# Two pieces of prompt work, then two value tiles, in the value pass of an attention kernel

## The chip, the cores and the metric

The kernel runs on one core of a Trainium2 chip. The metric is the device time in microseconds (us) of one execution, all inputs and outputs in the chip's memory. TensorE (PE) does the matrix products, with its weight loads shown apart as PEld; VectorE (DVE), ScalarE (ACT) and GpSimd (POOL) do the rest; SyncE (SP) and ACT issue the transfers (DMA) that the change touches. The engines run in order, each its own list of instructions, and wait for each other on semaphores.

## The reference

The reference is one step of a two-layer decoder: a diagonal state-space layer, then a layer of sparse attention, for a prompt of 256 tokens and for 8 samples of one token each. Only the attention is touched. It has 16 heads of 128 in 4 groups, and three branches that are weighted by gates: compressed keys, selected blocks, and a window.

```python
def nsa_mixer(hn, pos, kv, w_q, w_gate, b_gate, w_o):
    ...
    o_cmp, p_grp = cmp_branch(q, pos, kv['k_cmp'], kv['v_cmp'])
    idx, ok = select_blocks(p_grp, pos, kv['n_slc'])
    o_slc = kv['slc_fn'](q, pos, idx, ok)
    o_win = kv['win_fn'](q, pos)
    o = gates[:, :, 0] * o_cmp + gates[:, :, 1] * o_slc + gates[:, :, 2] * o_win
    return o.reshape(bsz, t, N_HEADS * HEAD_DIM) @ w_o
```

Each branch is a masked softmax: scores of the queries against the keys, less their maximum, exponential, divided by the sum, times the values. All is float32.

## The kernel before, in words

The attention runs two jobs at once. The samples' job streams the cached keys, then the cached values, through a ring of slots in on-chip memory: a tile is 128 rows of 1024 numbers, 512 KB. The value pass has 84 tiles, t = 80 to 163, or v = 0 to 83: 16 of the window, 64 of selected pages, 4 of compressed values. `values_pe` multiplies one tile: 8 instructions, each with 4 columns of probabilities as its weights and 128 columns of values moving, four of them side by side for the four groups (L2486). The trace counts two records for each of these instructions, 16 for a tile.

The prompt's job is cut into 24 items k: two halves of the queries (items 0 to 11, and 12 to 23), four groups, three branches. Items with k divisible by 3 have 15 compressed keys; the others have 128 keys in the first half and 256 in the second. An item passes through the engines in this order:

- scores on PE, `prompt_scores_pe`, L2303;
- on DVE the mask and the negative maximum, `prompt_mask_dve`, L2347 to L2355;
- on ACT four exponentials, `prompt_exp_act`, L2391;
- on DVE the probabilities, `prompt_probs_dve`, L2366 to L2377;
- on PE the turning of the probabilities, `prompt_turn_pe`, L2317;
- on ACT their copy out of PSUM, `prompt_take_act`, L2400;
- on PE the outputs, `prompt_outputs_pe`, L2329, and after each third item a copy on DVE, L2383.

The order of all this is written out by hand with v as the beat. In `beside_values_pe`, beat v = 3k has the scores of item k + 2, beat 3k + 1 turns item k, beat 3k + 2 has the outputs of item k - 1. Six extra pieces of the samples' job stand at v = 6, 8, 9, 16, 22 and 28. DVE has the probabilities of item k + 1 at beat 3k and then the mask of item k + 2 at beat 3k + 1. ACT has at beat 3k + 2 first the copy of item k, then the exponentials of item k + 2; behind every beat it issues half of the load that goes into the slot which tile v leaves, and for that it waits until PE has done tile v (`att_used`). SP issues the other half. Scores of item k wait until the mask of the item that last used their PSUM bank has read it, which for the items of 256 keys and those behind them is item k - 1.

The ring has 11 slots. The last four tiles, t = 160 to 163, come from a scratch tensor (L2051), all issued by SP, into the slots that tiles 150 to 153 leave; the first weight slab of the output projection is issued by SP between t = 160 and t = 161. Then the accumulated sample outputs are turned (L2593) and the output projection begins (L429).

Of the kernel before, what the change touches and what calls it, by code (L numbers as in the profile page):

```python
# [20 lines left out]
D, TP, TS, DEPTH = 2048, 256, 8, 2  # L21
# [88 lines left out]
def trunk_kernel(nc, io, out):  # L110
# [1863 lines left out]
    WK, SK, WV, SV, CV, TILES = 0, 16, 80, 96, 160, 164  # L1974
    SV_ALL = WV
# [31 lines left out]
    def tile_slot(t):  # L2007
        return TILE_SLOT[t]
# [50 lines left out]
    def wait_tile(pe, t):  # L2059
        done, base = TILE_READY[tile_slot(t)]  # L2060
        pe.wait_ge(done, base + 32 * (TILE_TURN[t] + 1))
# [19 lines left out]
    def gates_pe(pe):  # L2081
        pe.wait_ge(wg_split, 1)
        pe.wait_ge(free_a, by_name["o"].groups)
        for k in range(KC):
            if k == 10:
                own_rows_pe(pe)
            nc.tensor.matmul(PSUM[:, GATE_BANK, 0:T], WGH[:, k, :], XH[:, k, :], start=k == 0, stop=False)
            nc.tensor.matmul(PSUM[:, GATE_BANK, 0:T], WGH[:, k, :], XL[:, k, :], start=False, stop=False)
            last = nc.tensor.matmul(PSUM[:, GATE_BANK, 0:T], WGL[:, k, :], XH[:, k, :], start=False, stop=k == KC - 1)
        last.then_inc(gates_done, 1)  # L2090
# [202 lines left out]
    def prompt_scores_pe(pe, k):  # L2293
        qt, g, br = item = ITEMS[k]
        if k == 0:
            pc_dve.wait(pe, "k rows")
            pc_act.wait(pe, "v rows")
            pe.wait_ge(rope_done, len(ROPED))
        elif scores_before(k):
            pe.wait_ge(sc_used, scores_before(k))  # L2300
        for r in range(HREP):
            keys = KCP[:, g * NCMPP:(g + 1) * NCMPP] if br == 0 else KVT[:, 2 * br, g, 0:keys_of(item)]
            last = nc.tensor.matmul(score_view(k)[:, r, :], QT[:, HREP * g + r, qt * P:(qt + 1) * P], keys, start=True, stop=True)  # L2303
        last.then_inc(sc_done, 1)
# [6 lines left out]
    def prompt_turn_pe(pe, k):  # L2311
        pe.wait_ge(pr_done, k + 1)
        if k >= 1:
            pe.wait_ge(pt_taken, k)
        for kc, w in parts_of(k):
            for r in range(HREP):
                last = nc.tensor.transpose(PSUM[0:w, PROBS_BANK + kc, r * P:(r + 1) * P], prompt_rows(k)[:, r, kc * P:kc * P + w], IDENT[:, :])  # L2317
        last.then_inc(pt_done, 1)

    def prompt_outputs_pe(pe, k):  # L2320
        qt, g, br = ITEMS[k]
        parts = parts_of(k)
        pe.wait_ge(pt_taken, k + 1)
        o = k // 3
        if br == 0 and o >= 1:
            pe.wait_ge(po_used, o)
        for kc, w in parts:
            v = VCP[0:w, g, :] if br == 0 else VNAT[0:w, br - 1, kc, g * DH:(g + 1) * DH]
            last = nc.tensor.matmul(PSUM[:, OUT_BANK, :], v, PTP[0:w, k % 2, kc, :], start=br == 0 and kc == 0,  # L2329
                                    stop=br == 2 and kc == len(parts) - 1)  # L2330
        last.then_inc(pv_done, 1)
# [62 lines left out]
    def prompt_take_act(act, k):  # L2394
        n = keys_of(ITEMS[k])
        act.wait_ge(pt_done, k + 1)
        if k >= 2:
# [11 lines left out]
    sp_act = Steps("sp_act", ["cmp exp", "cmp turned kept", "block scores kept", "cmp gated kept", "win exp", "win new exp",  # L2409
                              "slc exp", "slc new exp", "slc kept 0", "slc kept 2"])  # L2410
    sp_dve = Steps("sp_dve", ["cmp negmax", "cmp probs", "new taken", "sums taken", "cmp gated", "win negmax", "win probs",
                              "win kept", "slc negmax", "slc probs", "new probs", "new kept", "new added",
                              "slc kept 1", "slc kept 3", "out"])
    ch_dve = sem("ch_dve")
    chain = [0]
    KSTEPS, VSTEPS = SV_ALL - WK, TILES - SV_ALL
# [10 lines left out]
    def turn_pe(pe, u):  # L2427

        wait_tile(pe, WK + u)
        if u == 1:  # L2430
            pe.wait_ge(gate_sig, 1)
            pe.wait_ge(part_done, 1)
        for e in range(2):
            if u >= 2:
                pe.wait_ge(kt_taken[e], u - 1)
            for g in range(G):
                at = 512 * e + g * DH
                last = nc.tensor.transpose(PSUM[:, 2 * (u % 2) + e, g * P:(g + 1) * P], TILE[:, tile_slot(WK + u), at:at + DH], IDENT[:, :])  # L2438
            last.then_inc(att_used, 1)
# [37 lines left out]
    def values_pe(pe, t):  # L2477
        wait_tile(pe, t)
        for e in range(2):
            if t < CV:  # L2480
                m, b = divmod(t - (WV if t < SV else SV), TS)
                probs, rows = (STW if t < SV else SCT)[:, 2 * m + e, :], P
            else:
                b, probs, rows = 2 * (t - CV) + e, PCS[0:NCMP, 2, :], NCMP
            for g in range(G):
                last = nc.tensor.matmul(PSUM[ROWS * g:ROWS * g + HREP, ACC_BANK + b // 4, b % 4 * P:(b % 4 + 1) * P],  # L2486
                                        probs[:, ROWS * g + HREP * b:ROWS * g + HREP * (b + 1)],
                                        TILE[0:rows, tile_slot(t), 512 * e + g * DH:512 * e + (g + 1) * DH],
                                        start=False, stop=False, skip_group_check=True)
            last.then_inc(att_used, 1)  # L2490
# [45 lines left out]
    def beside_values_pe(pe, v):  # L2536

        k, stage = divmod(v, 3)
        if stage == 0 and k + AHEAD_OF_VALUES < len(ITEMS):
            prompt_scores_pe(pe, k + AHEAD_OF_VALUES)  # L2540
        if stage == 1 and k < len(ITEMS):
            prompt_turn_pe(pe, k)
        if stage == 2 and 1 <= k <= len(ITEMS):
            prompt_outputs_pe(pe, k - 1)
        if v == 6:
            sp_dve.wait(pe, "new probs")
            for k in range(2):
                last = nc.tensor.transpose(PSUM[0:32, SPARE_BANK, k * P:(k + 1) * P], RTW[:, k, :], IDENT[:, :])
            sp_pe.made_by(last, "new turned")
        if v == 8:  # L2550
            sp_dve.wait(pe, "new kept")
            for k in range(2):
                last = nc.tensor.matmul(PSUM[:, SPARE_BANK, 2 * P:3 * P], SNAT[:, 3 + 2 * k, :], RTK[0:32, k, :], start=k == 0, stop=k == 1)
            sp_pe.made_by(last, "new values")
        if v in TURNED_AT:
            q = TURNED_AT.index(v)
            if q == 0:
                sp_dve.wait(pe, "new added")
            elif q % 2:
                sp_act.wait(pe, f"slc kept {q - 1}")  # L2560
            else:
                sp_dve.wait(pe, f"slc kept {q - 1}")
            for j in range(4):
                last = nc.tensor.transpose(PSUM[:, SPARE_BANK, j * P:(j + 1) * P], S2[:, (4 * q + j) * P:(4 * q + j + 1) * P], IDENT[:, :])
            sp_pe.made_by(last, f"slc turned {q}")

    def attention_pe(pe):
        gates_pe(pe)
        compressed_scores_pe(pe)
        turn_pe(pe, 0)  # L2570
        for u in range(KSTEPS):
            if u + 1 < KSTEPS:
                turn_pe(pe, u + 1)
            scores_pe(pe, u)
            beside_keys_pe(pe, u)
        pe.wait_ge(sc_used, AHEAD_OF_VALUES)
        for bank in range(2):
            nc.tensor.matmul(PSUM[:, ACC_BANK + bank, :], ZERO[:, 0:P], ZERO[:, :], start=True, stop=False, skip_group_check=True)
        for e in range(2):
            pe.wait_ge(kt_taken[e], KSTEPS)  # L2580
        for v in range(VSTEPS):
            t = SV_ALL + v
            beside_values_pe(pe, v)
            if t == WV:
                sp_dve.wait(pe, "win kept")
            if SV <= t < CV and (t - SV) % (2 * TS) == 0:
                q = (t - SV) // (2 * TS)
                (sp_dve if q % 2 else sp_act).wait(pe, f"slc kept {q}")
            values_pe(pe, t)
        for b in range(TS):  # L2590
            if b % 4 == 0:
                pe.wait_ge(vo_taken[b // 4], 1)
            last = nc.tensor.transpose(PSUM[:, b // 4, b % 4 * P:(b % 4 + 1) * P], VO[:, b // 4, b % 4 * P:(b % 4 + 1) * P], IDENT[:, :])  # L2593
        sp_pe.made_by(last, "out turned")
# [559 lines left out]
```

## Time and profile before

| what | value |
|---|---|
| median of 3 runs | 3226.36 us (3226.16 to 3226.61) |
| the profiled execution, its own time | 3226.72 us |
| its span in the trace | 3224.7 us |
| PE busy | 3167.0 us, 98% of the span |
| DVE busy | 1994.4 us, 62% |
| ACT busy | 1553.1 us, 48% |
| value pass, first piece to last value tile | 2107.2 to 2239.3 us in the span |

Times inside the trace count from the start of the span. A row of the timeline gives the start, the busy time, the engine with its line, and how many records were merged into it. A matrix product's busy time overlaps the next one's, so the distance from one start to the next is what a group costs.

### The profile page before, as it was taken

What the parts mean: (1) busy time and instruction counts of PE and PEld (TensorE: products, weight loads), DVE (VectorE), ACT (ScalarE), POOL (GpSimd) and SP (SyncE); (2) the same over time, 40 slices, a digit from 0 to 9 for tenths busy, and PEclk for the clock granted to TensorE, in tenths of its full rate; (3) what the DMA queues carried; (4) which work ended last, traced back from release to release, by engine and by line L of the source; (5) the groups of instructions that cost most, each with busy time, mean ns of one, the idle gap of its engine ahead of it and who ended that gap; (6) DMA issues with size and microseconds to landing.
All of it is one profiled execution on the core that took longest, in us unless ns stands there. A gap on an engine that the chain in (4) does not pass through costs nothing.

```text
span 3224.7 us, 68739 instructions
## 1 busy us (share of the span) xinstructions
PE 3167.0 (98%) x27708; PEld 3034.7 (94%) x27708; DVE 1994.4 (62%) x2283; ACT 1553.1 (48%) x1929; POOL 520.4 (16%) x476
## 2 busy tenths in 40 slices
PE   7999999999999999999999999999999999999998
PEld 6999899899999999999999997866999999999998
DVE  7998888865655544555675546465655554555566
ACT  4555555644544444444554533354554444444454
POOL 5666666600000000000000006000000000000000
PEclk9999999999999999999999999999999999999999
DMA  6455555466565556665556659898556555656553
GB/s 183 150 160 163 164 157 155 136 188 185 171 193 181 183 183 191 181 183 184 181 183 183 183 179 314 282 353 264 181 182 183 175 190 182 183 176 189 183 181 127
DMA packets 384389, 608.39 MB, mean 189 GB/s; under 512 B 52537, under 2 KB 144987, under 8 KB 383883
## 3 DMA queue, kind: packets, MB, share of 16 engines
q1 hardware_dynamic: 351738, 539.06, 53.5%
q10 hardware_dynamic: 29392, 60.86, 5.5%
q0 software_dynamic: 3024, 5.22, 0.5%
q8 instruction: 162, 2.65, 0.3%
q14 instruction: 73, 0.59, 0.1%
HBM read 594.83 MB, written 26.94 MB: 193 GB/s over the span
## 4 chain that ended last, share of the span: by engine, by line
PE 93%; DVE 3%; issue 1%; ACT 1%; DMA 1%; POOL 1%; SPq 0%; DVEq 0%; ACTq 0%; POOLq 0%
PE psum L429 23%; PE psum L431 23%; PE psum L430 23%; PE psum L1081 4%; PE psum L1082 3%; PE psum L1083 3%; PE psum L1060 3%; PE psum L2438 2%; PE psum L2448 1%; PE psum L2486 1%; PE psum L1138 1%; PE psum L2303 1%; PE psum L2329 1%; ACT state_ri L1226 1%; PE psum L2317 0%
## 5 line engine op out<-in xcount | busy, mean ns | idle before, releaser
L396 DVE TENSOR_TENSOR w_rest<-w_raw,w_head 128x1024 fp32r<-128x1024 f32 x776 | 973.0, 1265 | 945.3 <-ACT w_head L392 944.4
L392 ACT ACTIVATE w_head<-w_raw 128x1024 fp32r<-128x1024 f32 x776 | 909.6, 1183 | 945.4 <-PE psum L431 936.0
L429 PE MATMUL psum<-act_head,w_head 128*128 128x264 f32 x4224 | 1205.2, 285 | 1.6 <-DVE act_rest L2896 1.6
L431 PE MATMUL psum<-act_head,w_rest 128*128 128x264 f32 x4224 | 1200.9, 284 | 0.0
L430 PE MATMUL psum<-act_rest,w_head 128*128 128x264 f32 x4224 | 1199.9, 284 | 0.0
L429 PEld LDWEIGHTS psum<-act_head,w_head 128*128 128x128 f32 x4224 | 821.9, 195 | 2.4 <-issue 2.0
L430 PEld LDWEIGHTS psum<-act_rest,w_head 128*128 128x128 f32 x4224 | 822.4, 195 | 0.1
L431 PEld LDWEIGHTS psum<-act_head,w_rest 128*128 128x128 f32 x4224 | 821.8, 195 | 0.0
L429 PE MATMUL psum<-hid_head,w_head 128*128 128x264 f32 x1408 | 400.6, 284 | 0.0
L431 PE MATMUL psum<-hid_head,w_rest 128*128 128x264 f32 x1408 | 399.9, 284 | 0.0
L430 PE MATMUL psum<-hid_rest,w_head 128*128 128x264 f32 x1408 | 399.5, 284 | 0.0
L1819 POOL TENSOR_TENSOR hid_rest<-prod_val,hid_head 128x1056 f32 x22 | 54.4, 2471 | 1717.9 <-ACT hid_head L1780 1717.9
L1081 PE MATMUL psum<-rows_head,w_head 128*128 128x256 f32 x1024 | 301.3, 294 | 12.0 <-ACT state_ri L1226 5.1
L1082 PE MATMUL psum<-rows_rest,w_head 128*128 128x256 f32 x1024 | 290.9, 284 | 0.0
L1083 PE MATMUL psum<-rows_head,w_rest 128*128 128x256 f32 x1024 | 290.8, 284 | 0.0
L430 PEld LDWEIGHTS psum<-hid_rest,w_head 128*128 128x128 f32 x1408 | 273.7, 194 | 0.0
L429 PEld LDWEIGHTS psum<-hid_head,w_head 128*128 128x128 f32 x1408 | 273.5, 194 | 0.0
L431 PEld LDWEIGHTS psum<-hid_head,w_rest 128*128 128x128 f32 x1408 | 273.5, 194 | 0.0
L1217 ACT ACTIVATE rows_head<-psum 128x512 fp32r<-128x512 f32 x256 | 139.7, 596 | 209.0 <-PE psum L1060 208.9
L1081 PEld LDWEIGHTS psum<-rows_head,w_head 128*128 128x128 f32 x1024 | 194.8, 190 | 19.9 <-DVE rows_rest L1385 10.6
L1082 PEld LDWEIGHTS psum<-rows_rest,w_head 128*128 128x128 f32 x1024 | 195.3, 191 | 0.0
L1083 PEld LDWEIGHTS psum<-rows_head,w_rest 128*128 128x128 f32 x1024 | 195.2, 191 | 0.0
(433 smaller groups left out, 3990.4 us busy)
## 6 DMA issues: line engine op xcount, KB each, us to landing
w_raw<-in_ffn_w_gate SPq DMA_DIRECT2D x176, 512.0 KB, 4.4
w_raw<-in_ffn_w_up SPq DMA_DIRECT2D x176, 512.0 KB, 4.5
w_raw<-in_ffn_w_down SPq DMA_DIRECT2D x176, 512.0 KB, 3.7
w_raw<-in_cache_cmp_k SPq DMA_DIRECT2D x256, 128.0 KB, 2.6
w_raw<-in_cache_cmp_v SPq DMA_DIRECT2D x256, 128.0 KB, 2.6
w_raw<-in_ssm_w_glu SPq DMA_DIRECT2D x64, 512.0 KB, 4.4
w_raw<-in_ple_w_gate SPq DMA_DIRECT2D x64, 512.0 KB, 4.1
w_raw<-in_kv_w SPq DMA_DIRECT2D x48, 512.0 KB, 3.8
```

The source lines that it names most:

```text
L392: nc.scalar.activation(pairs(WH, u), tiles_of(RAW, u), ACT.Copy).then_inc(head_done, 1)
L396: nc.vector.tensor_tensor(pairs(WL, u), tiles_of(RAW, u), pairs(WH, u).bitcast(F32), ALU.subtract).then_inc(rest_done, 1)
L429: nc.tensor.matmul(o, wh, head, start=k == 0, stop=False)
L430: nc.tensor.matmul(o, wh, rest, start=False, stop=False)
L431: last = nc.tensor.matmul(o, wl, head, start=False, stop=k == UK * kunits - 1)
L1060: last = nc.tensor.transpose(PSUM[:, n % 2, q * P:(q + 1) * P], RAW[:, u, 256 * q + g * DH:256 * q + (g + 1) * DH], IDENT[:, :])
L1081: nc.tensor.matmul(o, WH[:, part, w], hi, start=t == 0, stop=False)
L1082: nc.tensor.matmul(o, WH[:, part, w], lo, start=False, stop=False)
L1083: last = nc.tensor.matmul(o, WL[:, part, w], hi, start=False, stop=t == TAPS - 1)
L1217: nc.scalar.activation(head_rows(k, m // 2, m % 2), page_rows(n), ACT.Copy).then_inc(cmp_head, 1)
L1819: nc.gpsimd.tensor_tensor(HL[:, ds(4 * i, 4), :], ZB[:, :, :], HH[:, ds(4 * i, 4), :].bitcast(F32), ALU.subtract).then_inc(hl_done, 1)
L2438: last = nc.tensor.transpose(PSUM[:, 2 * (u % 2) + e, g * P:(g + 1) * P], TILE[:, tile_slot(WK + u), at:at + DH], IDENT[:, :])
```

## The change

Only PE's order in the value pass changes. Before, each beat was one beat's pieces, then one tile. Now two beats' pieces come first, and then both tiles. What PE waits for ahead of each tile stays with the tile. The lists of ACT, DVE, SP and POOL are as before.

```diff
-        for v in range(VSTEPS):
-            t = SV_ALL + v
+        for v in range(0, VSTEPS, 2):
             beside_values_pe(pe, v)
-            if t == WV:
-                sp_dve.wait(pe, "win kept")
-            if SV <= t < CV and (t - SV) % (2 * TS) == 0:
-                q = (t - SV) // (2 * TS)
-                (sp_dve if q % 2 else sp_act).wait(pe, f"slc kept {q}")
-            values_pe(pe, t)
+            beside_values_pe(pe, v + 1)
+            for t in (SV_ALL + v, SV_ALL + v + 1):
+                if t == WV:
+                    sp_dve.wait(pe, "win kept")
+                if SV <= t < CV and (t - SV) % (2 * TS) == 0:
+                    q = (t - SV) // (2 * TS)
+                    (sp_dve if q % 2 else sp_act).wait(pe, f"slc kept {q}")
+                values_pe(pe, t)
```

The first place is the middle of the second half, beats 50 to 53, on PE. `x8` of L2486 is one tile; L2329 is an outputs piece, L2303 scores, L2317 turning. Before:

```order
L2329 MATMUL psum<-probs_t_p,v_cmp_p 128x512
L2486 MATMUL psum<-tiles,scores_st 4x128 x8
L2303 MATMUL psum<-kv_t,q_t 128x256 x4
L2486 MATMUL psum<-tiles,scores_st 4x128 x8
L2317 MATMUL psum<-ident,scores_p_149 128x128 x8
L2486 MATMUL psum<-tiles,scores_st 4x128 x8
L2329 MATMUL psum<-probs_t_p,v_rows 128x512 x2
L2486 MATMUL psum<-tiles,scores_st 4x128 x8
```

The same beats on PE after the change:

```order
L2329 MATMUL psum<-probs_t_p,v_cmp_p 128x512
L2303 MATMUL psum<-kv_t,q_t 128x256 x4
L2486 MATMUL psum<-tiles,scores_st 4x128 x16
L2317 MATMUL psum<-ident,scores_p_149 128x128 x8
L2329 MATMUL psum<-probs_t_p,v_rows 128x512 x2
L2486 MATMUL psum<-tiles,scores_st 4x128 x16
```

The tile of beat 52 stood right behind the turning piece (L2317) of its own beat; now an outputs piece (L2329 x2) stands between them. The tile of beat 50 now stands behind the scores of beat 51.

The second place is the end of the pass on PE, from the turning of item 22 on, as a difference:

```order
 L2317 MATMUL psum<-ident,scores_p 128x128 x8
 L2486 MATMUL psum<-tiles,scores_st 4x128 x8
+L2486 MATMUL psum<-tiles,scores_st 4x128 x16
 L2329 MATMUL psum<-probs_t_p,v_cmp_p 128x512
 L2486 MATMUL psum<-tiles,scores_st 4x128 x16
 L2317 MATMUL psum<-ident,scores_p_149 128x128 x8
-L2486 MATMUL psum<-tiles,scores_st 4x128 x8
 L2329 MATMUL psum<-probs_t_p,v_rows 128x512 x2
-L2486 MATMUL psum<-tiles,scores_st 4x128 x24
+L2486 MATMUL psum<-tiles,scores_st 4x128 x32
 L2329 MATMUL psum<-probs_t_p,v_rows 128x512 x2
```

Tile 150, whose slot takes t = 160, moves from ahead of the outputs of item 22 to behind them. In the whole pass the tiles stood in 70 runs between pieces; now they stand in 37.

## Rows read from the trace of the kernel before

**Rows 1.** Busy time by stretch, core 0: length, busy of each engine, PEclk, DMA share, GB/s.

```profile
2108.00:2228.00 120.00, 119.23 (x1565) 73.10 (x1563) 73.53 (x193) 57.23 (x211) 0.00 (x0) 1.00 0.93 325
...
2244.00:2249.00 5.00, 5.00 (x24) 5.00 (x24) 4.44 (x9) 5.00 (x12) 0.00 (x0) 0.50 0.48 170
```

**Rows 2.** Timeline of PE late in the pass: start, busy, engine, line, out<-in, records.

```profile
2218.67 1.06 PE L2486 MATMUL psum<-tiles,scores_st 128*4 128x128 f32 x32
2219.66 1.09 PE L2317 MATMUL psum<-ident,scores_p 128*128 128x128 f32 x8
2220.68 0.62 PE L2486 MATMUL psum<-tiles,scores_st 128*4 128x128 f32 x16
2221.23 1.12 PE L2329 MATMUL psum<-probs_t_p,v_cmp_p 15*128 15x512 f32 x2
```

**Rows 3.** Timeline of PE early in the pass, two turning pieces.

```profile
2116.84 0.66 PE L2317 MATMUL psum<-ident,scores_p 128*128 128x128 f32 x4
2117.42 0.62 PE L2486 MATMUL psum<-tiles,scores_wt 128*4 128x128 f32 x16
...
2130.91 0.66 PE L2317 MATMUL psum<-ident,scores_p 128*128 128x128 f32 x4
2131.40 0.60 PE L2564 MATMUL psum<-ident,scores_s 128*128 128x128 f32 x4
```

**Rows 4.** Timeline of DVE: masks of items 4, 7, 13 to 16, 23; last probabilities.

```profile
2119.01 0.68 DVE L2347 TENSOR_TENSOR scores_p<-psum,causal 128x512 f32<-128x512 f32 x1
...
2131.44 0.68 DVE L2347 TENSOR_TENSOR scores_p<-psum,causal 128x512 f32<-128x512 f32 x1
...
2158.74 1.22 DVE L2347 TENSOR_TENSOR scores_p<-psum,causal 128x1024 f32<-128x1024 f32 x1
...
2165.32 1.22 DVE L2347 TENSOR_TENSOR scores_p<-psum,causal 128x1024 f32<-128x1024 f32 x1
...
2171.89 0.21 DVE L2347 TENSOR_TENSOR scores_p<-psum,cmpvis 128x60 f32<-128x60 f32 x1
...
2175.16 1.22 DVE L2347 TENSOR_TENSOR scores_p<-psum,causal 128x1024 f32<-128x1024 f32 x1
...
2216.24 1.22 DVE L2347 TENSOR_TENSOR scores_p<-psum,causal 128x1024 f32<-128x1024 f32 x1
...
2221.67 1.23 DVE L2377 TENSOR_TENSOR scores_p<-scores_p,soft_small 128x1024 f32<-128x1024 f32 x1
```

**Rows 5.** Timeline: tile 141, copy of item 20, exponentials of items 22 and 23.

```profile
2210.18 0.62 PE L2486 MATMUL psum<-tiles,scores_st 128*4 128x128 f32 x16
...
2211.47 1.02 ACT L2400 ACTIVATE probs_t_p<-psum 128x1024 f32<-128x1024 f32 x1 [3.47 <-PE psum L2486]
...
2212.39 0.50 ACT L2391 ACTIVATE scores_p<-scores_p,soft_small 128x256 f32<-128x256 f32 x1
...
2218.95 0.51 ACT L2391 ACTIVATE scores_p<-scores_p,soft_small 128x256 f32<-128x256 f32 x1 [0.87 <-DVE soft_small L2355]
```

**Rows 6.** Timeline of PE: scores of item 16, with the idle time before them.

```profile
2172.16 1.99 PE L2303 MATMUL psum<-kv_t,q_t 128*128 128x256 f32 x8 [0.41 <-DVE scores_p L2347]
```

**Rows 7.** The chain that ended last, 2222 to 2246 us: start, length, what.

```profile
2223.34 1.02 PE psum L2317 x8
...
2224.91 1.92 PE psum L2329 x4
...
2230.36 7.84 DMA tiles<-cmp_v_scratch
```

**Rows 8.** Timeline of SP's queue at the end of the pass: issue of transfers.

```profile
2224.97 0.90 SPq L2051 DMA_DIRECT2D tiles<-cmp_v_scratch  x2
2225.97 0.52 SPq L380 DMA_DIRECT2D w_raw<-in_nsa_w_o  x1
2227.44 3.79 SPq L2051 DMA_DIRECT2D tiles<-cmp_v_scratch  x6
```

## The prediction, as it was put on record before the change was run

> **What bounds the kernel now.** I read the page first (PE is busy 98% of the span, so time can only be had where PE itself spends or waits), then the busy time of the touched stretch, then PE's timeline in it, then the timelines of DVE and ACT, and last the chain of waits at the stretch's end. In the value pass PE is busy 119.23 of 120 us at full clock, and DVE and ACT look loose at 73.5 and 57.2 us [rows 1]. The DMA engines move 325 GB/s there at a share of 0.93. So at first sight the pass is PE's, and whatever makes PE's list shorter is gained in full. The reader should look twice, at three things.
>
> First, PE's list can be shortened. A single value tile costs 0.55 us from its start to the next piece (2220.68 to 2221.23), two tiles in a row 0.99 us (2218.67 to 2219.66) [rows 2]. The second tile costs 0.44 us, and 0.11 us is what going from tiles to pieces costs once.
>
> Second, the prompt's softmax has a beat of its own that 61% and 48% of busy time hide. Item k's probabilities and item k + 1's mask follow each other on DVE, then the maximum, then ACT's exponentials, then DVE again, and neither engine works ahead on another item. One group of three items in the second half takes 16.42 us from mask to mask (2158.74 to 2175.16), of which an item of 256 keys takes 6.58 and the one of compressed keys 3.27 [rows 4]. In that stretch PE already waits for it once: the scores of item 16 stood 0.41 us for a mask [rows 6].
>
> Third, the pass ends in a transfer. The last of the four tiles from scratch is issued at 2230.36 and lands 7.84 us later, and the tile on PE follows [rows 7].
>
> **The change part by part.** *Fewer switches on PE.* There are 70 runs of tiles before and 37 after, so 33 runs go. Each saves 0.11 us on the tiles' side [rows 2]. On the pieces' side, a turning piece of 4 records costs 0.58 us ahead of a tile (2116.84 to 2117.42) and 0.49 ahead of another piece (2130.91 to 2131.40) [rows 3]: 0.09 saved. One of 8 records costs 1.02 us (2219.66 to 2220.68) [rows 2], against 2 x 0.58 for two separate ones, which makes 0.14. The other kinds of piece I have not isolated; I take 0.09 for all. PE's list gets shorter by 33 x 0.20 = 6.6 us. If pieces next to each other save nothing it is 33 x 0.11 = 3.6, if all save 0.14 it is 33 x 0.25 = 8.3.
>
> [...]
>
> *The first half.* Up to the mask of item 4 (2119.01) DVE and ACT are busy with the samples' own softmax, and nothing that PE does sooner helps. From there to the mask of item 13 (2158.74) pass 39.73 us, three groups; the first, to 2131.44, took 12.43 [rows 4]. As no wait for PE shows in it I take it for the softmax's own pace: 3 x 12.43 = 37.3, and 0.6 for one copy of turned probabilities on DVE that falls into the second group. So at most 39.73 - 37.9 = 1.8 us are to be had, though PE by then has dropped 17 runs, 17 x 0.20 = 3.4 us. The rest PE spends waiting for masks. I take 1.7.
>
> *The second half.* From the mask of item 13 to the end of the last probabilities (2221.67 + 1.23 = 2222.90) pass 64.16 us. At the softmax's own pace it would be 3 x 16.42 + 6.58 + 6.66 = 62.5 (6.66 is the last item, 2216.24 to 2222.90) [rows 4]. So the most that a faster PE can bring here is 1.7 us, where PE's list gets 16 x 0.20 = 3.2 us shorter.
>
> *What the new order costs.* ACT's list is in order: the copy of item k stands behind the load that waits for tile v = 3k + 1, and the exponentials of item k + 2 behind that copy. For odd k that tile now comes after one more piece, the outputs of item k - 1. Where ACT is late already, this holds up the softmax. It bites where scores that wait for a mask are followed by long pieces, and that is item 19: its scores (beat 51) wait for the mask of item 18, and then PE has to do them (1.92 us), two tiles (0.99), the turning of item 17 (1.02), the outputs of item 16 (1.92) and tile 132 (0.62) before ACT can start its copy 0.67 later and the exponentials 0.92 after that (2210.80 to 2211.47 to 2212.39) [rows 2, 5, 7]; the 1.92 of the scores is their row of 1.99 less the overlap [rows 6]. Sum 8.06, less 0.1 as pieces abut. The softmax alone would need from the end of the mask of item 18 to the exponentials of item 19 3.27 - 0.21 + 2.71 = 5.8 us (2.71 is 2216.24 to 2218.95) [rows 4, 5]. The hold is about 2.1 us, once; the same walk for items 15, 17, 21 and 23, with smaller pieces in it, gives from nothing to 0.2. So the second half gains 1.7 and loses 2.1 + 0.1: 0.5 us worse. The turning of item 23, at 2223.3 now, comes 1.7 - 0.5 = 1.2 us sooner.
>
> *The end.* The slot for t = 160 is left by tile 150. Before, that tile ran right behind the turning of item 23; now the outputs of item 22 stand ahead of it, 1.92 us [rows 7]. SP then issues t = 160, a weight slab and t = 161 to 163 in one row: 0.90 + 0.52 + 3.79 and 0.2 of gaps, 5.4 us [rows 8]. Before, the first issue stood 1.7 us after the turning began, and the last ended 7.9 us after it (2223.3 to 2231.23), since it waited for tile 151 in between. Now it is 1.02 + 1.92 + 0.62 = 3.6 us to the first issue and 9.0 to the last. If issuing sets the landing, 1.0 of the 1.2 us is lost; if the full DMA queues set it (7.84 us for a transfer of 256 KB says that one waits in line), none is. I take half, 0.5.
>
> *After the pass* PE goes at half clock, 0.50 from 2244 to 2249 [rows 1], since it stood for the last tiles. It will stand as long or a little longer; I cost this at nothing, with 1 us either way in the range.
>
> **Sum.** -1.7 + 0.5 + 0.5 = -0.7 us. The profiled execution took 3226.72 us, 2.0 more than its span, and 0.36 more than the median; I put the sum against the median: 3225.7 us.
>
> **The rivals.**
> *PE's saving is paid in full*, each switch that goes shortens the pass: 3226.4 - 6.6 = 3219.8, with 8.3 it would be 3218.1. For it: PE 98% busy, DVE and ACT with room. Against it: the wait of rows 6, and a softmax that has only 1.8 + 1.7 us of slack over 104 us. The scores would have to come much ahead of their masks, which the banks forbid. [...]
> *Pieces next to each other save nothing, and ACT is held for every odd item.* Then PE has 17 x 0.11 = 1.9 us by item 13, as much as the extra outputs piece of 1.05 us for odd items and its wait at the first turnings take from it: no gain there. In the second half the hold of item 19 stays, and those of items 14 and 18 grow to some 0.4 each: 1.7 - 2.1 - 0.8 = 1.2 us worse. With the 1.0 of the end this is 2.2 us and up: 3226.4 + 2.4 = 3228.8. It decides if the pieces' side saves under 0.05 us. For it: outputs and scores next to each other are not in the trace. Against it: the 0.49 of rows 3.
> *The last transfers set the end whatever PE does*: 3226.4, no change. For it: a transfer of 256 KB that takes 7.84 us stood in line [rows 7]. Against it: its issue waits for tiles of PE, and those come sooner.
>
> **How the numbers follow.** Chances: the forecast, a gain of 0.2 to 2 us, 0.55; full saving 0.07; held for every odd item 0.26; no change 0.12. The predicted time is the likeliest case's, 3225.7. The range runs from 3222.5 (PE waits less than I think, half of its saving comes through) to 3229.2 (the slower rival with its 0.4 for the clock). 0.2%, about what a measurement of this kernel can tell from no change, is 6.5 us. Only the full saving reaches beyond it: faster 0.06, slower 0.02, and 0.92 within.
>
> **What would show it.** Right: the PE timeline shows pairs of 0.99 us and PE idle ahead of L2303 for L2347, for items 13, 15, 16, 19, 21 and 22, some 0.4 to 1.3 us each; masks of items 13 and 16 still 16.4 us apart; some 8.5 us from the mask of item 19 to that of item 20; the exponentials of item 19 right behind a copy. SP's issues of t = 160 to 163 in one row. Wrong: groups of the second half under 16.4 us apart, or PE without waits in the pass, which would mean that the softmax's beat isn't its own; value pairs of 1.1 us; a wait of PE for a value tile from the pages, which would mean that the transfers fall behind; or a clock below 1.00 inside the pass.

## The result, and the profile after

| what | before | after |
|---|---|---|
| median | 3225.81 us (3224.47 to 3228.02, 22 runs) | 3230.57 us (3228.48 to 3233.70, 22 runs) |
| ratio to before, 95% interval | | 1.0014 (1.0009 to 1.0020) |
| the profiled execution, its own time | 3226.72 us | 3230.62 us |
| its span | 3224.7 us | 3228.7 us |

The change costs 4.8 us, by the ratio 0.14%. That is inside the 0.2% called no change. But the interval excludes 1, the time lies above the range that was forecast (3222.5 to 3229.2), and the sign is the other one: 0.7 us of gain was forecast.

The two profiled spans differ by 4.0 us. The first mask of the pass (item 2) starts at 2108.42 us before and at 2108.60 after, so 0.2 us of shift comes in from ahead. From that mask to the turning of item 23 pass 114.85 us before (to 2223.27) and 117.75 after (to 2226.35): 2.9 us more in the pass. From that turning to the start of the last value tile pass 14.98 us before (to 2238.25) and 16.18 after (to 2242.53): 1.2 more at the end. Behind the start of the last tile both kernels take the same time (986.4 and 986.2 us to the end of the span).

Windows of the kernel after: length, busy time of PE, PEld, DVE, ACT, POOL, then the granted clock, DMA share and GB/s. The first row answers to that of [rows 1].

```profile
2108.00:2228.00 120.00, 113.51 (x1501) 77.17 (x1500) 73.61 (x194) 57.03 (x211) 0.00 (x0) 0.97 0.89 315
...
2166.00:2168.00 2.00, 1.98 (x41) 1.72 (x41) 1.97 (x3) 0.55 (x3) 0.00 (x0) 1.00 0.94 346
2168.00:2172.00 4.00, 4.00 (x18) 2.12 (x18) 2.26 (x8) 1.53 (x7) 0.00 (x0) 0.51 0.86 266
2172.00:2174.00 2.00, 2.00 (x33) 1.22 (x26) 0.00 (x0) 0.44 (x1) 0.00 (x0) 0.50 0.18 62
2174.00:2176.00 2.00, 2.00 (x8) 1.69 (x8) 0.22 (x1) 1.74 (x9) 0.00 (x0) 0.77 0.85 288
```

PE's busy time in the pass fell from 119.23 to 113.51 us in 120: that much PE now stands, and yet the pass got longer. DVE and ACT do what they did. And the clock, 1.00 over the whole pass before, has a stretch of some 7 us at 0.50, from 2168 to 2175. Transfers thin out in it as well (62 GB/s), where before moved 346 GB/s in the same 2 us: the slots come free later.

Where PE stands is in its timeline after, with the idle time ahead of a group and who ended it in brackets:

```profile
2112.45 0.63 PE L2317 MATMUL psum<-ident,scores_p 128*128 128x128 f32 x4 [0.57 <-ACT probs_t_p L2400]
2121.06 0.66 PE L2564 MATMUL psum<-ident,scores_s 128*128 128x128 f32 x4 [0.42 <-DVE new_values L2800]
...
2154.76 1.99 PE L2303 MATMUL psum<-kv_t,q_t 128*128 128x256 f32 x8 [0.66 <-DVE scores_p L2347]
...
2166.02 1.06 PE L2303 MATMUL psum<-k_cmp_p,q_t 128*128 128x15 f32 x8 [1.44 <-DVE scores_p L2347]
2167.01 1.06 PE L2486 MATMUL psum<-tiles,scores_st 128*4 128x128 f32 x32
2168.00 1.93 PE L2317 MATMUL psum<-ident,scores_p 128*128 128x128 f32 x8
2169.85 2.07 PE L2329 MATMUL psum<-probs_t_p,v_cmp_p 15*128 15x512 f32 x2
2171.85 1.89 PE L2486 MATMUL psum<-tiles,scores_st 128*4 128x128 f32 x32
2173.67 2.59 PE L2303 MATMUL psum<-kv_t,q_t 128*128 128x256 f32 x8
...
2190.84 1.99 PE L2303 MATMUL psum<-kv_t,q_t 128*128 128x256 f32 x8 [0.78 <-DVE scores_p L2347]
...
2203.82 1.06 PE L2303 MATMUL psum<-k_cmp_p,q_t 128*128 128x15 f32 x8 [1.01 <-DVE scores_p L2347]
...
2209.39 1.99 PE L2303 MATMUL psum<-kv_t,q_t 128*128 128x256 f32 x8 [0.46 <-DVE scores_p L2347]
...
2222.08 1.06 PE L2317 MATMUL psum<-ident,scores_p 128*128 128x128 f32 x8 [0.96 <-ACT probs_t_p L2400]
```

The waits for L2347 stand ahead of the scores of items 13, 15, 19, 21 and 22, between 0.46 and 1.44 us. A pair of tiles costs 0.99 us (2167.01 to 2168.00). Then the same rows show the half clock: the turning piece 1.85 us instead of 1.02 [rows 2], the pair of tiles 1.82 instead of 0.99. PE had stood 1.44 us just before. The wait ahead of item 16 of [rows 6] is gone, because this time PE is the late one there.

The masks of items 19 and 20 on DVE before:

```profile
2192.02 1.22 DVE L2347 TENSOR_TENSOR scores_p<-psum,causal 128x1024 f32<-128x1024 f32 x1
...
2198.98 1.22 DVE L2347 TENSOR_TENSOR scores_p<-psum,causal 128x1024 f32<-128x1024 f32 x1
```

The masks after, items 13 to 16, 19, 20 and 23, answer to these two and to those of [rows 4]:

```profile
2157.76 1.22 DVE L2347 TENSOR_TENSOR scores_p<-psum,causal 128x1024 f32<-128x1024 f32 x1
...
2164.75 1.22 DVE L2347 TENSOR_TENSOR scores_p<-psum,causal 128x1024 f32<-128x1024 f32 x1
...
2171.32 0.21 DVE L2347 TENSOR_TENSOR scores_p<-psum,cmpvis 128x60 f32<-128x60 f32 x1
...
2177.03 1.22 DVE L2347 TENSOR_TENSOR scores_p<-psum,causal 128x1024 f32<-128x1024 f32 x1
...
2193.83 1.22 DVE L2347 TENSOR_TENSOR scores_p<-psum,causal 128x1024 f32<-128x1024 f32 x1
...
2202.55 1.22 DVE L2347 TENSOR_TENSOR scores_p<-psum,causal 128x1024 f32<-128x1024 f32 x1
...
2219.21 1.22 DVE L2347 TENSOR_TENSOR scores_p<-psum,causal 128x1024 f32<-128x1024 f32 x1
```

Four readings, each the distance of two starts. Item 13 comes 1.0 us sooner than before (2157.76 against 2158.74), 1.16 with the shift taken off. From 15 to 16 it is 5.71 us, where [rows 4] had 3.27. From 19 to 20 it is 8.72 us, where before had 6.96. From 13 to 16 it is 19.3 us, not 16.4.

What held item 16 is on ACT. Its timeline after shows the copy of item 13. It stands behind a load that waits for tile 120 (the pair at 2171.85), which PE does at half clock; behind the copy come the exponentials of item 15 (15 columns each):

```profile
2173.56 1.02 ACT L2400 ACTIVATE probs_t_p<-psum 128x1024 f32<-128x1024 f32 x1 [4.02 <-PE psum L2486]
...
2174.48 0.30 ACT L2391 ACTIVATE scores_p<-scores_p,soft_small 128x15 f32<-128x15 f32 x1
```

Item 15's mask was through at 2171.53. The exponentials of item 12, of the same size, began 0.5 us behind their mask, so those of item 15 came some 2.5 us after they could have.

At the end, SP's queue after, in answer to [rows 8]:

```profile
2229.75 0.90 SPq L2051 DMA_DIRECT2D tiles<-cmp_v_scratch  x2
2230.74 1.33 SPq L380 DMA_DIRECT2D w_raw<-in_nsa_w_o  x1
2232.12 4.18 SPq L2051 DMA_DIRECT2D tiles<-cmp_v_scratch  x6
```

All four scratch tiles and the slab are issued in one row now; the last issue ends 9.95 us after the turning of item 23 began (2236.30 less 2226.35). The chain that ended last, after, in answer to [rows 7]:

```profile
2226.35 1.06 PE psum L2317 x8
2227.41 1.72 PE psum L2329 x4
...
2235.76 6.73 DMA tiles<-cmp_v_scratch
```

The transfer at its end is issued 9.4 us behind the turning, where it was 7.0 before (2223.34 to 2230.36), and lands in 6.73 us instead of 7.84: of 2.4 us more, half is given back.

### The profile page after: what moved, and what is told of

Same layout as the page of the kernel before. It is cut to its first block, busy times and chain, and to the rows that moved or that the text cites. A ratio compares the mean times of both kernels' runs of the same rounds, so it can differ in the third digit from the quotient of the medians.

```text
span 3228.7 us, 68739 instructions
## 1 busy us (share of the span) xinstructions
PE 3166.1 (98%) x27708; PEld 3042.4 (94%) x27708; DVE 1994.6 (62%) x2283; ACT 1553.3 (48%) x1929; POOL 520.0 (16%) x476
## 4 chain that ended last, share of the span: by engine, by line
PE 91%; DVE 4%; ACT 2%; issue 1%; DMA 1%; POOL 1%; ACTq 0%; DVEq 0%; POOLq 0%; SPq 0%
PE psum L429 23%; PE psum L431 23%; PE psum L430 23%; PE psum L1081 4%; PE psum L1083 3%; PE psum L1082 3%; PE psum L1060 3%; PE psum L2438 2%; PE psum L2448 1%; PE psum L1138 1%; PE psum L2486 1%; PE psum L2329 1%; PE psum L2303 1%; DMA taps_first<-in_cmp_k_w 1%; ACT state_ri L1226 0%
## 5 line engine op out<-in xcount | busy, mean ns | idle before, releaser
L1081 PE MATMUL psum<-rows_head,w_head 128*128 128x256 f32 x1024 | 302.1, 295 | 11.7 <-ACT state_ri L1226 5.1
```

Source lines behind the costliest of these rows:

```text
L1081: nc.tensor.matmul(o, WH[:, part, w], hi, start=t == 0, stop=False)
```

## The experiments

The theory from these rows: the softmax's own pace turns PE's saving into waits; a wait lets TensorE's clock fall for a while, and while it is down PE holds up the softmax. Rivals: the loss comes from the new order itself, with the tile that ACT waits for behind one more piece; or it is the end alone; or abutting pieces save nothing. Every kernel was run 11 times beside its own runs of before.

| kernel | median us | range us | ratio to before, 95% |
|---|---|---|---|
| `fill15` | 3227.12 | 3224.63 to 3229.30 | 1.0003 (0.9994 to 1.0012) |
| `first` | 3225.14 | 3223.95 to 3226.84 | 0.9997 (0.9988 to 1.0006) |
| `second` | 3229.63 | 3225.94 to 3232.59 | 1.0010 (1.0001 to 1.0019) |
| `tail1` | 3229.85 | 3228.22 to 3231.84 | 1.0013 (1.0004 to 1.0022) |
| `open_before` | 3225.53 | 3223.70 to 3228.16 | 1.0000 (0.9991 to 1.0009) |
| `open_after` | 3221.39 | 3220.38 to 3224.18 | 0.9986 (0.9977 to 0.9995) |
| `act1` | 3222.31 | 3220.61 to 3224.34 | 0.9989 (0.9980 to 0.9998) |
| `act1_before` | 3225.81 | 3224.32 to 3227.98 | 0.9999 (0.9990 to 1.0008) |
| `filltail` | 3227.09 | 3224.72 to 3228.59 | 1.0002 (0.9993 to 1.0011) |
| `fillmany` | 3227.06 | 3225.24 to 3229.22 | 1.0004 (0.9995 to 1.0013) |
| `open_tail` | 3220.94 | 3219.47 to 3221.77 | 0.9984 (0.9975 to 0.9993) |
| `all_three` | 3218.86 | 3218.03 to 3220.89 | 0.9978 (0.9969 to 0.9987) |
| `fill1921` | 3229.73 | 3227.75 to 3232.54 | 1.0013 (1.0004 to 1.0022) |
| `after_again` | 3230.36 | 3228.71 to 3232.08 | 1.0013 (1.0004 to 1.0022) |

Before had medians of 3226.06 to 3226.36 beside them. A difference of less than a microsecond between medians is not read as one. The fall of the clock that the rows above show, a stretch at 0.50 inside the pass, is called the fall from here on, and a late start of ACT's exponentials a hold.

### Is it the clock? Fill the gap ahead of item 15

```diff
+            if k + AHEAD_OF_VALUES in (15,):
+                sp_dve.wait(pe, "slc kept 3")
+                for _ in range(4):
+                    nc.tensor.matmul(PSUM[:, SPARE_BANK, :], ZERO[:, 0:P], ZERO[:, :], start=True, stop=True)
```

> The changed kernel with four extra products of zeros (128x512, into a PSUM bank that is no longer used) on TensorE ahead of the scores of item 15, where it stood idle for 1.44 us; they fill about 1.0 us of that wait and cost nothing while PE waits anyway. Theory A (that idle time made the granted clock fall to 0.50 for 7 us behind it, and the slow turning and outputs held ACT's copy and all that follows): the clock stays at 1.00 behind item 15, masks of items 15 and 16 are some 3.7 us apart in place of 5.71, and the time falls by 1.8 to 2.4 us against the changed kernel (to about 0.07% over the kernel before). Theory B (the hold of ACT behind the displaced tiles is what costs, the clock is a side show): the time stays within 0.5 us of the changed kernel's, 0.14% over before.

The wait on DVE ahead of the zeros did not hold PE, and the bank that they go into is no longer used. The kernel took 3227.12 us, 3.5 us less than after, where 1.8 to 2.4 less were expected, and its trace has no stretch below 1.00 in the pass. PE's timeline of `fill15`, the wait of item 15 and those behind it:

```profile
2165.76 1.06 PE L2303 MATMUL psum<-k_cmp_p,q_t 128*128 128x15 f32 x8 [0.51 <-DVE scores_p L2347]
...
2171.33 1.99 PE L2303 MATMUL psum<-kv_t,q_t 128*128 128x256 f32 x8 [0.46 <-DVE scores_p L2347]
...
2187.99 1.99 PE L2303 MATMUL psum<-kv_t,q_t 128*128 128x256 f32 x8 [0.87 <-DVE scores_p L2347]
...
2200.97 1.06 PE L2303 MATMUL psum<-k_cmp_p,q_t 128*128 128x15 f32 x8 [1.01 <-DVE scores_p L2347]
...
2206.54 1.99 PE L2303 MATMUL psum<-kv_t,q_t 128*128 128x256 f32 x8 [0.46 <-DVE scores_p L2347]
...
2219.23 1.06 PE L2317 MATMUL psum<-ident,scores_p 128*128 128x128 f32 x8 [0.96 <-ACT probs_t_p L2400]
```

The masks of items 15, 16, 19 and 20 of `fill15` on DVE:

```profile
2171.06 0.21 DVE L2347 TENSOR_TENSOR scores_p<-psum,cmpvis 128x60 f32<-128x60 f32 x1
...
2174.57 1.22 DVE L2347 TENSOR_TENSOR scores_p<-psum,causal 128x1024 f32<-128x1024 f32 x1
...
2190.98 1.22 DVE L2347 TENSOR_TENSOR scores_p<-psum,causal 128x1024 f32<-128x1024 f32 x1
...
2199.70 1.22 DVE L2347 TENSOR_TENSOR scores_p<-psum,causal 128x1024 f32<-128x1024 f32 x1
```

From 15 to 16 it is 3.51 us, so the 5.71 of after held 2.2 us that belong to the fall. From 19 to 20 it is 8.72 us with or without it: that hold is the order's. Work that computes nothing made the kernel faster, and what it changed is PE's idle time ahead of item 15, now 0.51 us. As far as its trace goes this kernel is the change without the fall: 0.8 us above before, which no measurement here can tell from nothing.

### The control: fill elsewhere, and run after again

```diff
-            if k + AHEAD_OF_VALUES in (15,):
+            if k + AHEAD_OF_VALUES in (19, 21):
```

> The control of fill15: the same products of zeros in the changed kernel, but ahead of the scores of items 19 and 21, with the wait of 1.44 us ahead of item 15 left open. If it is the idle time ahead of item 15 that lets the clock fall: as the changed kernel, some 4 us over before, mean clocks of 0.992 to 0.994. If any products of zeros in the pass, or the falls behind items 19 and 21, made the difference of fill15: 3226.5 to 3227.5.

The same zeros at other places bring less than a microsecond (3229.73 us), as the theory has it. PE in `fill1921`, and its windows:

```profile
2165.05 1.22 PE L2303 MATMUL psum<-k_cmp_p,q_t 128*128 128x15 f32 x8 [1.57 <-DVE scores_p L2347]
```

```profile
2164.00:2168.00 4.00, 2.95 (x40) 2.13 (x40) 2.98 (x4) 1.58 (x8) 0.00 (x0) 0.73 0.73 254
2168.00:2172.00 4.00, 4.00 (x48) 2.81 (x45) 2.25 (x7) 0.62 (x4) 0.00 (x0) 0.85 0.82 259
```

The clock falls right behind the unfilled gap of item 15, as in after, though for 3.5 us only, and the masks of items 15 and 16 are 5.05 us apart.

The kernel after was then run once more, unchanged.

> The changed kernel as it is, once more, beside fill1921 on the same chip: 4 to 5 us over before, mean clock 0.992 to 0.994 in every execution, and in its trace at least one stretch of 6 to 7 us in the pass at a granted clock of 0.50 that follows an idle time of TensorE of over 1 us.

The time came back (3230.36 us), the place did not. PE's wait for item 21 in `after_again`:

```profile
2201.81 1.06 PE L2303 MATMUL psum<-k_cmp_p,q_t 128*128 128x15 f32 x8 [1.02 <-DVE scores_p L2347]
```

Its windows, around item 15 and around item 21:

```profile
2168.00:2172.00 4.00, 3.70 (x66) 2.24 (x57) 2.35 (x6) 2.14 (x9) 0.00 (x0) 1.00 0.79 251
...
2204.00:2208.00 4.00, 4.00 (x19) 2.04 (x22) 2.25 (x7) 1.32 (x6) 0.00 (x0) 0.50 0.85 250
2208.00:2212.00 4.00, 4.00 (x39) 2.94 (x30) 0.44 (x2) 2.18 (x9) 0.00 (x0) 0.66 0.59 182
```

Behind the same 1.44 us ahead of item 15 the clock stayed at 1.00 this time; it fell behind the 1.02 us of item 21, and the masks of items 21 and 22 moved 5.67 us apart instead of 3.50. So a fall can come at such a gap and is not bound to one of them, and it cost the same at both places: 5.71 - 3.51 and 5.67 - 3.50, 2.2 us each.

How often it happens can be judged only roughly, by the mean granted clock over the span, which every execution has. A stretch of 7 us at half clock takes 3.5 / 3228 = 0.001 off it, one step of its last digit, so it says nothing of a single execution: the profiled ones of `second` and `fill1921` had a fall and 0.995 all the same. Taken together, of the 33 executions of after (11 of them `after_again`) one has 0.995 and none more. Of 120 of before 84 have 0.995 or 0.996, and of the 11 of `fill15` 7 have 0.995. That speaks for a fall in most executions of after; it is shown for the two that were profiled. The expectation of 0.992 to 0.994 in every execution was missed by one of `after_again` and by two of `fill1921`.

More filling, at items 13, 15, 19 and 21, changes nothing over `fill15` (3227.06 us):

> The changed kernel with the four products of zeros ahead of the scores of items 13, 15, 19 and 21, the four places where its trace shows PE idle for 0.66 to 1.44 us. They last about 1 us, so at items 13 and 19 they cost 0.1 to 0.3 us. If idle time of PE is what lets the clock fall in some executions: less spread than with the one filled wait (3224.6 to 3229.3), no mean clock under 0.994 in any run, and a median 0 to 0.8 us under that of fill15 (3227.1). If the falls have nothing to do with these waits: the same spread and median, or 0.5 us more.

### Which half of the pass?

```diff
-            beats += [(v, v + 1)]
+            beats += [(v, v + 1)] if v < 30 else [(v,), (v + 1,)]
```

The line shown is `first`; `second` has `v >= 30`, where item 12 and with it the second half begins.

> Pairs in beats 0 to 29 only, beats 30 to 83 as before. If the first half is bound by PE and gains until the mask of item 13, as the traces show (-1.2 us there), and the second half keeps its own pace as before: faster than before by 0.5 to 1.2 us, no clock fall. If the gain of the first half is lost again as PE then waits for masks in the second half: no difference.

> Beats 0 to 29 as before, pairs in beats 30 to 83. The other part of the change: the loss should all be here. By theory A and B both the hold of item 19 (+1.8) and the end (+1.2) stay; with the clock falling ahead of item 15 again +2.4 more: 4 to 5.5 us slower than before. If PE arrives later at item 15, its wait is shorter (under 1 us) and the clock may hold: then 2.5 to 3.5 us slower.

`first` 3225.14 us, `second` 3229.63: all that can be measured of the loss comes from the pairs in the second half, where the gaps and the hold of item 19 are. In `second` the clock fell behind the wait of item 21 (granted 0.50 from 2204 to 2208). At 3.3 us over its own before it stays under the 4 to 5.5 that were expected with a fall. `first` was expected to have no fall and had one, from 2171.3 to 2174.7, behind its wait of 0.78 us for item 16. In its trace the masks of items 16 and 17 are 7.70 us apart instead of 6.58, and the profiled execution took 3226.67 us, 1.5 more than the kernel's median. So the fall wasn't free in that execution. Whether the others of `first` had it is not known.

### The end

```diff
-            beats += [(v, v + 1)]
+            beats += [(v, v + 1)] if v < 68 else [(v,), (v + 1,)]
```

> The changed kernel with beats 68 to 83 in the order of before, so that tile 150 runs right behind the turning of item 23 again and SP issues t = 160 earlier. If issuing in one row sets when the last tiles land: 0.8 to 1.3 us faster than the changed kernel. If the full DMA queues set it: no difference.

In the trace the way from the turning of item 23 to the last tile is 14.66 us instead of 16.18, so the 1.2 us of the trace are the order's and go away with it. The median is 3229.85 us, 0.7 less than after; each against its own runs of before, 3.5 over instead of 4.8. The trace has two falls of 3.4 us each, behind the waits of items 15 and 19, which together made its pass 0.6 us longer than that of after.

> The filled wait ahead of item 15 and beats 68 to 83 in the order of before, together. From the trace of fill15 (turning of item 23 0.2 us later than in before, last tile 1.4 later): if the place of tile 150 costs the end its 1.2 us, this is 1.0 to 1.4 us faster than fill15 and equal to before within 0.5 us. If the DMA queues set the end: as fill15.

Filling and single beats at the end together: 14.92 us for the end in the trace, and a median of 3227.09, the same as `fill15`. This expectation was missed. The end is shorter in one profiled execution, and the medians do not show it. Why is open.

### Is it the softmax's own pace? Open the ring

If items follow each other at DVE's and ACT's pace since neither works ahead, DVE has to take the next mask before the waiting probabilities. This changes DVE's list alone:

```diff
-        if stage == 0 and k >= 1 and k + AHEAD_OF_VALUES <= len(ITEMS):
-            prompt_probs_dve(dve, k + AHEAD_OF_VALUES - 1)
...
+        if stage == 1 and k >= 1 and k + AHEAD_OF_VALUES <= len(ITEMS):
+            prompt_probs_dve(dve, k + AHEAD_OF_VALUES - 1)
```

The added lines stand behind the mask of item k + 2. It was put on the kernel before and on the one after.

> The kernel before with one exchange on DVE alone: the mask of item k + 2 comes ahead of the probabilities of item k + 1, so the softmax of one item no longer has to end before that of the next begins. PE's order is as before. If PE sets the pace of the order before but for one wait of 0.41 us, almost nothing changes: 0 to 0.6 us faster than before. If the softmax's own beat already held it back (theory: it had 3.5 us of slack over the pass): the same 0.4.

> The same exchange on DVE under the changed order of PE. If it is the softmax's beat that keeps PE's shorter list from paying, the waits for L2347 ahead of L2303 go, no clock fall inside the pass, the turning of item 23 comes 6 to 7 us sooner than in the kernel before, the end takes 1.2 back, and the time is 4.5 to 6 us under before. If the saving on the switches is not real, or the transfers of the pages bound the pass (wait of PE for tiles<-in_cache_slc_v): within 1 us of before.

Before, the exchange brings nothing (3225.53 us): there PE's list is the bound. With the pairs it brings 9 us (3221.39; no fall in the trace), 4.1 less than `open_before`. So PE's shorter list is worth something as soon as the softmax can follow. The waits of PE in the pass of `open_after` (total us, times, longest) name no mask any more; in after the mask's line had 4.4 us in 5 waits:

```profile
PE psum L2317 <- ACT probs_t_p L2400: 1.7, 3, 1.0
PE psum L2317 <- DVE scores_p L2377: 0.5, 2, 0.3
```

This also measures the saving itself. From the mask of item 2 to the turning of item 23 `open_before` takes 114.41 us (2108.42 to 2222.83) and `open_after` 109.54 (2107.55 to 2217.09), 4.87 less. PE stands 0.4 us in the first and 2.2 in the second. So by this pair of traces its work got 4.87 + 1.8 = 6.7 us shorter. "Abutting pieces save nothing" is ruled out. The clock stays at 1.00 in that pass.

### Is the hold of item 19 ACT's place?

```diff
-        if stage == 2:
+        if stage == 1:
```

This puts ACT's copy and exponentials one beat earlier, ahead of the load that waits for tile 3k + 1.

> The changed kernel with ACT's copy of item k and its exponentials of item k + 2 one beat earlier in ACT's list, so that they no longer stand behind the load that waits for tile 3k + 1; DVE is as it was. Theory (the displaced tile holds ACT): the 8.72 us from the mask of item 19 to that of item 20 become 6.6, and the turning of item 23 comes 3 to 4 us sooner than in the kernel with the filled wait; with the end's 1.2 the time is 2 to 3 us under before, if the clock holds (PE still waits about 1.1 us ahead of item 15), else about as before. Rival (ACT's place in the list does not matter, the rounds of DVE and ACT are long in themselves): as the changed kernel, 4 us over before.

3222.31 us, 8.3 less than after and 4.8 less than `fill15`; its trace has no fall in the pass. This is 3.9 under its own before, where 2 to 3 were expected. The masks of items 19 and 20 in `act1`:

```profile
2188.44 1.22 DVE L2347 TENSOR_TENSOR scores_p<-psum,causal 128x1024 f32<-128x1024 f32 x1
...
2195.02 1.22 DVE L2347 TENSOR_TENSOR scores_p<-psum,causal 128x1024 f32<-128x1024 f32 x1
```

They are 6.58 us apart instead of 8.72, and each group of three items takes 16.42 us (2155.61 to 2172.03 to 2188.44 to 2204.86). That is the softmax's pace with no hold in it, as taken from [rows 4], and it shows that the hold was the place of ACT's work in its list. In `fill15`, ACT had the copy of item 17 end a wait of 5.24 us for a tile, and the exponentials of item 19 began at 2195.85 behind it, 4.87 us behind their mask; in `act1` they begin 2.71 us behind their mask and wait for DVE alone. The smaller holds go with it. In `fill15` the distances from mask to mask are longer than in `act1` behind items 5, 7, 9, 13, 15, 19 and 21 (by 0.40, 0.76, 0.30, 0.41, 0.24, 2.14 and 0.23 us), all of them odd, and behind no other by more than 0.02.

> The kernel before, PE's order and all, with ACT's copy and exponentials one beat earlier. Theory: in the old order the tile that ACT waits for stands right behind the turning, so nothing holds it up by more than 0.4 us and PE has its own pace; no difference, within 0.5 us. Rival: the gain of act1 (3.9 us) is ACT's alone and has nothing to do with the order of PE: 3 us or more under before.

On the kernel before the same edit brings 0.3 us at most (3225.81): there no tile was late enough for it to matter.

### All together

> The changed order of PE with the exchange on DVE (as open_after) and beats 68 to 83 in the order of before. If the end costs 1.2 us there too: about 1 us under open_after (3221.4), so 3220.3, 5.9 under before. If not: the same.

> As open_tail, and ACT's copy and exponentials one beat earlier too. The two changes of DVE and ACT take the same waits out of PE's way, so they do not add up: 0 to 0.8 us under open_tail. If ACT's place still held up the copies ahead of the turnings of items 22 and 23 (0.96 and 0.17 us in open_after): those waits go and it is 0.5 to 0.8.

`open_tail` takes 3220.94 us, 0.45 less than `open_after`, again less than the 1.2 of its trace (the end 14.72 instead of 15.91). `all_three` has the pairs up to v = 67, both edits and single beats at the end. At 3218.86 us it is 2.1 us under `open_tail`, where 0 to 0.8 were expected: 0.9 are waits of PE that went, the rest is open. It beats before by 7.3 us (ratio 0.9978, interval 0.9969 to 0.9987) and after by 11.7. PE waits in its pass, from the timeline:

```profile
2111.24 0.63 PE L2317 MATMUL psum<-ident,scores_p 128*128 128x128 f32 x4 [0.58 <-ACT probs_t_p L2400]
2115.44 0.66 PE L2317 MATMUL psum<-ident,scores_p 128*128 128x128 f32 x4 [0.22 <-DVE scores_p L2377]
...
2164.11 1.09 PE L2317 MATMUL psum<-ident,scores_p 128*128 128x128 f32 x8 [0.25 <-DVE scores_p L2377]
...
2211.54 1.09 PE L2317 MATMUL psum<-ident,scores_p 128*128 128x128 f32 x8 [0.28 <-DVE scores_p L2377]
```

That is 1.3 us of waits in all, none above 0.6. The pass takes 108.20 us to the turning of item 23 against 114.85 before, 6.65 less: about the full saving, though the pairs end at v = 67.

## Why the prediction was wrong, by its own steps

**What bounds the kernel: right.** The softmax's beat of 16.42 us for three items sets the second half once PE is faster. `act1` runs at exactly that, and `open_after` gains by breaking it (14.92 us for the same three items). PE's 98% did not mean that PE's time is the kernel's.

**PE's list 6.6 us shorter: right.** 6.7 by `open_before` and `open_after`. How it would go on was right too: pairs at 0.99 us, and waits for L2347 ahead of items 13, 15, 19, 21 and 22 of 0.46 to 1.44 us. Item 16, which the prediction also named, has its 0.46 us in `after_again` and `fill15`, where PE wasn't late for it.

**The first half, 1.7 us: mis-sized.** Item 13's mask came 1.16 us sooner. It comes 49.16 us behind that of item 2 in after and 47.67 in `act1`. The 1.5 us between them are holds of items 5, 7 and 9, the same kind that the prediction walked in the second half only. Its bound of 1.8 us was too low besides: the 0.6 us that it gave to a copy on DVE are not there in `act1`, where each group of this half takes 12.36 us.

**The second half, small holds mis-sized.** The hold of item 19 was right: 8.72 us from its mask to the next against some 8.5 forecast. For the other items the prediction had "from nothing to 0.2", and 0.1 in the sum. In `fill15`, where the clock stays up, the distances from item 13 to 23 exceed the softmax's own 6.58 and 3.27 by 0.41 (item 14), 0.24 (16), 2.15 (20) and 0.23 (22), 3.03 in all, against 1.66 in the kernel before. So the half is 1.4 us worse instead of 0.5. The largest of them, 0.41, is that of item 13, whose exponentials stand behind the copy of item 11; the walk left it out, though 13 is odd. `act1` has none of these holds.

**The clock inside the pass: the step that failed.** The prediction cost the clock at nothing, with 1 us either way, and looked for it only behind the pass. In its last part it lists "a clock below 1.00 inside the pass" as a sign that it is wrong; no term, rival or width stood for it. Yet it forecast itself six waits of up to 1.3 us in a row of work that had none above 0.41 [rows 6]. What the runs showed in its place: a fall of 7 us behind such a wait costs 2.6 us of distance in the traces (117.75 less 115.17 in `fill15`), more than half of the miss of 4.9; the medians of after and `fill15` differ by 3.5, and in the traces the rest lies outside the pass, 0.3 ahead of it and 0.7 behind the last tile. The fall costs that much since it comes where the softmax has no slack: for 7 us PE needs nearly twice the time for what it does, down to the tile that ACT waits for (1.82 us for a pair of tiles instead of 0.99, 1.85 for a turning piece instead of 1.02), and the exponentials of item 15 came 2.5 us late.

**The end, 0.5 us: 1.2 in the trace.** The bounds 0 and 1.0 were too tight. The six issues for t = 161 to 163 took 4.18 us, not 3.79, and the slab between 1.33 instead of 0.52. The medians of kernels with and without it differ by 0 to 0.7 (1.3 for `tail1`, if each is taken against its own runs of before), so what it costs on average is not settled.

**After the pass: right.** The stretch at half clock moves with the end of the pass (0.50 from 2236 to 2249 before and from 2240 to 2253 after) and costs what it cost before: from the start of the last tile to the end of the span pass 986.4 us before and 986.2 after.

**The rivals.** Full saving did not come, but what it needed is now known: `open_after` and `all_three` are that case. The slower rival named 3228.8, which is nearest to what was measured, but for a false reason. Its condition, that abutting pieces save nothing, is ruled out; what it had right in part was a hold of 0.4 us ahead of item 14's mask; the one that it named at item 18 is not there.

Sum of after's trace against before's: item 13 sooner by 1.2, the fall and the hold at item 16 later by 2.4, the hold of item 19 by 1.8, the rest by -0.1, makes 2.9; the end 1.2. With 2.6 of it taken off for the fall, 1.5 is left in the trace; the median of `fill15` is 0.8 over that of before.

**What stays open.** Which of the gaps lets the clock fall in a given execution, and in how many it falls; why it stays up at item 21 in the trace of `fill15`, where only the gap of item 15 was filled, while `after_again` fell there; and why the shorter end of `filltail` is not in its median.

## What to carry to other kernels

Before shortening the list of an engine that is busy 98% of the time, measure the round of the others: the distance between the same step of two items, against the sum of what must follow one another in it. If there is little slack, the time saved turns into gaps, and gaps of a microsecond on TensorE can cost more than what is left of the saving (here item 13 came 1.2 us sooner, and a fall of 7 us behind a gap of 1.44 us cost 2.6); open the round first (here the next mask ahead of the waiting probabilities, and ACT's copy ahead of a load's wait), then shorten. And walk for every item, not for the worst alone, what an in-order engine has behind the instruction that was moved.

## What the runs showed of the hardware

A stand of 0.8 to 1.6 us on TensorE, in a stretch where it was busy 94 to 98% of the time (112.88 of 120 us in `tail1`, 113.51 after, 117.83 in `first`), was followed by a fall of the granted clock to 0.50. It lasted about 7 us in after, behind the 1.44 us of item 15, and in `after_again` and `second`, behind the 1.02 and 1.01 us of item 21. It lasted about 3.4 us in `first`, `fill1921` and twice in `tail1`. Not each such gap does it: `fill15` still has 0.87, 1.01 and 0.96 us and no fall in its trace. With four products of zeros in the gap of item 15 the clock stayed at 1.00 in three traces (`fill15`, `filltail`, `fillmany`). One fall cost 2.6 us of distance where 7 us stood at 0.50 (after against `fill15`), and a short one 1.1 to 1.6, by the distance between the masks at it (7.70 us instead of 6.58 in `first`, 5.05 instead of 3.51 in `fill1921`, 10.34 instead of 8.72 in `tail1`).

A change of PE from 4-column tiles to full-width pieces and back cost about 0.2 us in this pass: 6.7 us less work with 33 runs fewer (`open_before` and `open_after`).
